# The first norm's weight as one row, spread over the partitions by TensorE, with the second half of x requested right behind it

## The chip, the cores and the metric

The kernel runs on one core of a Trainium2 chip. A core has TensorE (PE, matrix products), VectorE (DVE), ScalarE (ACT), GpSimd (POOL) and SyncE (SP), each with its own queue of instructions, taken in order. They meet through semaphores. SyncE writes the requests for all DMA transfers here. The metric is the time of one execution on the device, in microseconds, as the median of several runs.

## The reference

A decoder trunk of two layers over x with 256 tokens of width 1024, all in float32. The part that matters here is the first step of the first layer:

```python
def rms_norm(x, g):
    xf = x.astype(jnp.float32)
    y = xf * lax.rsqrt(jnp.mean(xf * xf, axis=-1, keepdims=True) + RMS_EPS)
    return (y * g.astype(jnp.float32)).astype(x.dtype)

for l in range(DEPTH):
    h = rms_norm(x, norm_mix[l])
    proj = h @ w_in[l]          # then three mixers (S5, NSA, stick-breaking), merge, output projection
    ...
    h = rms_norm(x, norm_ffn[l])
    x = x + conv_ffn(h, ...)
return rms_norm(x, norm_final)
```

`norm_mix[0]`, called the gain below, is a row of 1024 numbers by which every token's normed row is multiplied.

## The kernel before

Tokens lie on the 128 partitions, in two blocks t = 0 and 1 of 128 tokens; `xr[:, t, :]` holds a block's 1024 columns, in two halves h of 512. Each layer norms x into `xn`, transposes it on TensorE into `hh` and `hl` (each float32 value is split in a high part hh and a rest hl), and multiplies it by weight pieces that are split the same way into `wh` (ScalarE) and `wl` (VectorE). Weight chunks come through `ring`, three slots, each loaded again when VectorE has split what was in it. Every engine's order is written out by hand. `xn` and the gains are parts of one buffer, which the profile names `gate`.

At the start the order around the change is this.

SyncE requests the first half of x (block 0), the lambda rows (two requests) and step rows (two), the identity matrix (`kon`, 64 KB), the gain (`g_next`, read with a broadcast so that it lands on all 128 partitions, 512 KB), the second half of x (block 1), and then the chunks of the ring.

ScalarE squares a block as soon as it has landed and sums the squares (L1226), and takes the root (L1232). VectorE forms the bias of the root (`norm_bias`, L1562), waits for the lambda and step rows and spreads the latter (L1706), and norms the block (`norm_rows`: a reciprocal L1567, then for each half one scalar_tensor_tensor L1572, x times 1/root times gain). It does this for block 0, then block 1. Then it forms `hl` (L1578) and `wl` (L1556). The small computations for the S5 tables and the splits of further pieces come behind.

TensorE waits for the identity, runs ten products of the identity with itself into bank bY (`idle(10)`, L736, a warm-up whose results nobody reads), transposes block 0 when `xn_ready` says so (`turn_normed`, L795, banks bX0 and bX1), transposes the lambda rows (L820), runs four more such products, transposes block 1 (banks bA and bB), again four, and then starts the projection into the banks pj0 and pj1. A product of two plain float32 operands shows as two records in the profile, a transpose as one.

Of the kernel before, what the change touches and what calls it, by code (L numbers as in the profile page):

```python
# [20 lines left out]
ALU = mybir.AluOpType  # L21
# [3 lines left out]
P = 128  # L25
D = 1024
# [125 lines left out]
K_ID, K_ROT, K_TRI, K_NEG1 = 0, 128, 256, 384  # L152
# [72 lines left out]
def build(nc, x, norm_mix, w_in, ssm_lam_re, ssm_lam_im, ssm_log_step, ssm_b_re, ssm_b_im,  # L225
# [3 lines left out]
    with ExitStack() as ctx:  # L229
        def sb(name, shape, dtype=F32):  # L230
            return ctx.enter_context(nc.sbuf_tensor(name, shape, dtype))

        def bank(name):
            return ctx.enter_context(nc.psum_tensor(name, [P, 512], F32))
# [3 lines left out]
        def sem(name, per_round=0, start=0, rounds=DEPTH):  # L238
            t = Tally(ctx.enter_context(nc.semaphore(name)), name, per_round, start, rounds)
            tallies.append(t)  # L240
            return t
# [3 lines left out]
        kon = sb("kon", [P, K_ALL])  # L245
        xr = sb("xr", [P, NT, D])
# [7 lines left out]
        rstd = sb("rstd", [P, NT])  # L254
# [13 lines left out]
        kr = sb("kr", [P, 4, T])  # L268
# [42 lines left out]
                st[:, :, :].rearrange("p (c t) q -> p c (t q)", c=2)]  # L311
        s5xs = [s5x[:, :, :], bnat[:, :, :, :].rearrange("p c t i -> p c (t i)")]

        cv = work[:, 0]
        aT = work[:, 1]
        yt = work[:, 2]
# [23 lines left out]
        xn = gates[:, 2]  # L340
        g_next, g_ffn = gates[:, 1, 0], gates[:, 1, 1]
# [8 lines left out]
        pj = [bank(f"pj{i}") for i in range(2)]  # L350
# [3 lines left out]
        bB = bank("bB")  # L354
        bO = bank("bO")
        across_banks = [bX[0], bX[1], bA, bB]


        ident_in = sem("ident_in")
        consts_in = sem("consts_in")  # L360
        x_in = [sem(f"x_in{i}") for i in range(NT)]
        g_in = [sem(f"g_in{i}", 16, 16 if i else 0) for i in range(2)]
        setup = sem("setup")
        passed = sem("passed")
        out_sent = sem("out_sent")
# [153 lines left out]
        xd = x.rearrange("b (t p) d -> p (b t) d", p=P)  # L519
        od = out.rearrange("b (t p) d -> p (b t) d", p=P)  # L520

        def half(h):
            return slice(CH * h, CH * h + CH)
# [25 lines left out]
        @block.sync  # L549
        def _(sp):  # L550
            sp.dma_start(xr[:, 0, :], xd[:, 0, :]).then_inc(x_in[0].sem, 16)
            sp.wait_ge(setup.sem, 1)
            sp.sem_inc(passed.sem, 1)
            sp.dma_start(stP[L_RE:L_RE + DEPTH * ST, :], ssm_lam_re.rearrange("l (t w) p -> (l t) (w p)", w=2))\
# [3 lines left out]
            for l in range(DEPTH):  # L558
                sp.dma_start(lstep[L_ST + 32 * l:L_ST + 32 * l + ST, :],
                             ssm_log_step[l:l + 1].rearrange("l (t w) -> (l t) w", w=2)).then_inc(lam_in.sem, 16)  # L560
            sp.dma_start(kon[:, K_ID:K_ID + P], consts[:, K_ID:K_ID + P]).then_inc(ident_in.sem, 16)
            sp.dma_start(g_next, norm_mix[0:1, :].broadcast_to([P, D])).then_inc(g_in[1].sem, 16)
            sp.dma_start(xr[:, 1, :], xd[:, 1, :]).then_inc(x_in[1].sem, 16)

            def row(w, l):
                return w[bass.ds(l, 1)]
# [102 lines left out]
            for l in range(DEPTH):  # L669
# [34 lines left out]
                i = C_FFN  # L704
# [19 lines left out]
            n = 2 * DEPTH  # L724
# [9 lines left out]
        def _(pe):  # L734
            def mm(o, a, b, start, stop):
                return nc.tensor.matmul(o, a, b, start=start, stop=stop, skip_group_check=True)  # L736
# [62 lines left out]
            def turn_normed(n, t):  # L799
                for h in range(2):  # L800
                    pe.wait_ge(xn_ready.sem, xn_ready.at(n, 2 * t + h + 1))
                    turn(xn, t, h)
# [6 lines left out]
            def idle(n):  # L809

                for _ in range(n):
                    mm(bY[:, 0:P], ident, ident, True, True)

            pe.wait_ge(ident_in.sem, 16)
            idle(10)
            for l in range(DEPTH):
                turn_normed(2 * l, 0)
                if l == 0:
# [716 lines left out]
        def _(v):  # L1535
            TT, TS, STT = nc.vector.tensor_tensor, nc.vector.tensor_scalar, nc.vector.scalar_tensor_tensor

            for part in (stP, stA, stB, stC):
                nc.vector.memset(part, 0.0).then_inc(setup.sem, 1)
            nc.vector.memset(one[:, :], 1.0).then_inc(setup.sem, 1)  # L1540
# [24 lines left out]
            def norm_rows(n, t):  # L1565
                v.wait_ge(root_ready.sem, root_ready.at(n, t + 1))
                nc.vector.reciprocal(rstd[:, t:t + 1], rstd[:, t:t + 1]).then_inc(dve_step.sem, dve_step.up())  # L1567
                v.wait_ge(dve_step.sem, dve_step.last())
                g, gain = (g_in[0], g_ffn) if n % 2 else (g_in[1], g_next)
                v.wait_ge(g.sem, g.at(n // 2, 16) if n % 2 else g.at(n // 2, 0))  # L1570
                for h in range(2):
                    STT(xn[:, t, half(h)], xr[:, t, half(h)], rstd[:, t:t + 1], gain[:, half(h)], ALU.mult, ALU.mult)\  # L1572
                        .then_inc(xn_ready.sem, xn_ready.up())

            def turned_lo(l, n, t, h, k):
# [119 lines left out]
            for l in range(DEPTH):  # L1695
                n = 2 * l
# [5 lines left out]
                if l == 0:  # L1702
                    v.wait_ge(lam_in.sem, 64)
                    for w in range(DEPTH):
# [3 lines left out]
                            lstep[rows, :].rearrange("t (w o) -> t w o", o=1).broadcast_to([ST, 2, HD]))\  # L1708
                            .then_inc(step_row.sem, 1)
                norm_rows(n, 0)  # L1710
                if l:
                    x_down(l - 1, 1, 0)
# [4 lines left out]
                    split_lo(l, 2)  # L1717
                norm_bias(n, 1)
                norm_rows(n, 1)
                if l == 0:  # L1720
                    turned_lo(l, 1, 0, 0, 0)
# [182 lines left out]
                for q in range(SLOTS):  # L1904
                    f = q // 2
# [27 lines left out]
                    n = U_FILL + f  # L1933
# [15 lines left out]
                    if q in OS_SPLIT:  # L1949
                        n = OS_SPLIT[q]  # L1950
# [21 lines left out]
                n = 2 * l + 1  # L1972
# [6 lines left out]
                split_lo(l, S_FFN)  # L1979
                x_out(l, 0, 1)  # L1980
                norm_rows(n, 0)
                x_out(l, 1, 1)
                turned_lo(l, 9, 0, 0, 0)
# [60 lines left out]
            n = 2 * DEPTH  # L2044
# [184 lines left out]
```

## Time and profile before

| | us |
|---|---|
| median of 3 runs (993.08 to 993.66) | 993.47 |
| the profiled execution | 991.46 |
| its span, first to last instruction | 989.7 |
| TensorE busy | 953.2 |
| VectorE busy | 746.2 |
| ScalarE busy | 565.4 |
| GpSimd busy | 338.2 |

The page of the profile tells busy times and the chain that ended last. Its timeline gives, for each engine, the start and length of what it ran in microseconds from the span's start, and in brackets how long the engine sat idle before and what ended that. The windows tell busy times by stretch. Durations below are of the profiled execution.

### The profile page before, as it was taken

What the parts mean: (1) busy time and instruction counts of PE and PEld (TensorE: products, weight loads), DVE (VectorE), ACT (ScalarE), POOL (GpSimd) and SP (SyncE); (2) the same over time, 40 slices, a digit from 0 to 9 for tenths busy, and PEclk for the clock granted to TensorE, in tenths of its full rate; (3) what the DMA queues carried; (4) which work ended last, traced back from release to release, by engine and by line L of the source; (5) the groups of instructions that cost most, each with busy time, mean ns of one, the idle gap of its engine ahead of it and who ended that gap; (6) DMA issues with size and microseconds to landing.
All of it is one profiled execution on the core that took longest, in us unless ns stands there. A gap on an engine that the chain in (4) does not pass through costs nothing.

```text
span 989.7 us, 17232 instructions
## 1 busy us (share of the span) xinstructions
PE 953.2 (96%) x6447; PEld 819.5 (83%) x6447; DVE 746.2 (75%) x1240; ACT 565.4 (57%) x905; POOL 338.2 (34%) x267
## 2 busy tenths in 40 slices
PE   7899899999999999999999998999999999999997
PEld 6799666776878999999989986777777799999996
DVE  5989999995666776677865689999857676665666
ACT  6436665757454655555564466666664555555544
POOL 0111666671320563155401047568506001011010
PEclk9999999999999999999999999999999999999999
DMA  8963433344554765555468424233645345655551
GB/s 230 263 187 96 133 114 128 122 98 164 168 168 136 204 196 179 181 200 170 132 179 255 155 93 128 85 129 103 183 141 170 128 152 190 200 182 177 200 176 43
DMA packets 135864, 156.83 MB, mean 158 GB/s; under 512 B 16400, under 2 KB 103032, under 8 KB 135800
## 3 DMA queue, kind: packets, MB, share of 16 engines
q1 hardware_dynamic: 135800, 155.98, 50.7%
q8 instruction: 40, 0.66, 0.3%
q14 instruction: 24, 0.20, 0.1%
HBM read 154.92 MB, written 1.05 MB: 158 GB/s over the span
## 4 chain that ended last, share of the span: by engine, by line
PE 73%; DVE 16%; ACT 5%; issue 3%; POOL 2%; DMA 1%; SPq 0%; DVEq 0%; ACTq 0%; POOLq 0%; PEldq 0%
PE pj L736 52%; PE bX L736 6%; PE bA L736 5%; DVE wl L1556 5%; PE bB L736 4%; PE bY L1085 2%; DVE s5x L1885 1%; PE bY L736 1%; DVE work L1849 1%; DVE bnat L1885 1%; POOL s5h L2144 1%; PE bX L1074 1%; DVE gate L1572 1%; DVE hl L1578 1%; PE bO L736 1%
## 5 line engine op out<-in xcount | busy, mean ns | idle before, releaser
L1556 DVE TENSOR_TENSOR wl<-ring,wh 128x1024 fp32r<-128x1024 f32 (+1 forms) x276 | 365.0, 1326 | 136.4 <-ACT wh L1262 134.9
L1262 ACT ACTIVATE wh<-ring 128x1024 fp32r<-128x1024 f32 (+1 forms) x276 | 289.0, 1048 | 238.2 <-PE pj L736 201.4
L736 PE MATMUL pj<-hh,wh 128*128 128x256 f32 x1024 | 293.1, 286 | 6.7 <-DVE wl L1556 4.8
L736 PE MATMUL pj<-hl,wh 128*128 128x256 f32 x1024 | 289.7, 283 | 0.0
L736 PE MATMUL pj<-hh,wl 128*128 128x256 f32 x1024 | 289.7, 283 | 0.0
L736 PEld LDWEIGHTS pj<-hh,wh 128*128 128x128 f32 x1024 | 196.2, 192 | 11.3 <-issue 6.6
L736 PEld LDWEIGHTS pj<-hl,wh 128*128 128x128 f32 x1024 | 196.3, 192 | 1.2 <-issue 0.5
L736 PEld LDWEIGHTS pj<-hh,wl 128*128 128x128 f32 x1024 | 196.3, 192 | 0.0
L736 PE MATMUL pj<-wh,hl 128*128 128x512 f32 (+1 forms) x416 | 169.3, 407 | 10.3 <-ACT sbv L1249 4.9
L736 PE MATMUL pj<-wh,hh 128*128 128x512 f32 (+1 forms) x416 | 160.5, 386 | 0.0
L736 PE MATMUL pj<-wl,hh 128*128 128x512 f32 (+1 forms) x416 | 159.9, 384 | 0.0
L2182 POOL TENSOR_TENSOR work<-work 128x512 f32<-128x512 f32 x20 | 41.0, 2050 | 291.3 <-DVE work L1998 152.6
L736 PEld LDWEIGHTS pj<-wh,hl 128*128 128x128 f32 x416 | 78.5, 189 | 40.0 <-issue 11.3
L736 PEld LDWEIGHTS pj<-wh,hh 128*128 128x128 f32 x416 | 78.4, 188 | 16.4
L736 PEld LDWEIGHTS pj<-wl,hh 128*128 128x128 f32 x416 | 78.7, 189 | 12.8
L1998 DVE SCALAR_TENSOR_TENSOR work<-pj,par,work 128x254 f32<-128x254 f32 (+1 forms) x176 | 76.5, 475 | 13.4 <-ACT work L1480 8.3
L1480 ACT ACTIVATE work<-pj,par 128x256 f32<-128x256 f32 x88 | 44.2, 554 | 10.5 <-PE pj L736 10.5
L1351 ACT ACTIVATE work<-work,nm 128x128 f32<-128x128 f32 (+1 forms) x64 | 28.4, 444 | 31.4 <-DVE nm L1849 31.3
L2126 POOL TENSOR_TENSOR mr<-mr,work 128x512 f32<-128x512 f32 x16 | 31.9, 2008 | 32.7 <-DVE work L1614 32.7
L736 PE MATMUL bX<-wh,al 128*128 128x512 f32 x88 | 34.7, 395 | 0.3 <-DVE al L2033 0.3
L736 PE MATMUL bX<-wl,ah 128*128 128x512 f32 x88 | 34.5, 392 | 0.0
L736 PE MATMUL bX<-wh,ah 128*128 128x512 f32 x88 | 34.2, 389 | 0.0
(315 smaller groups left out, 1473.7 us busy)
## 6 DMA issues: line engine op xcount, KB each, us to landing
ring<-in_ffn_w_up SPq DMA_DIRECT2D x44, 1024.0 KB, 5.1
ring<-in_w_in SPq DMA_DIRECT2D x40, 1024.0 KB, 5.2
ring<-in_ffn_w_down SPq DMA_DIRECT2D x22, 1024.0 KB, 4.9
ring<-in_w_in SPq DMA_DIRECT2D x16, 512.0 KB, 5.3
ring<-in_w_branch SPq DMA_DIRECT2D x8, 1024.0 KB, 5.1
ring<-in_w_out SPq DMA_DIRECT2D x8, 1024.0 KB, 5.1
ring<-in_w_branch SPq DMA_DIRECT2D x8, 512.0 KB, 5.8
ring<-in_w_in SPq DMA_DIRECT2D x8, 256.0 KB, 5.1
```

The costliest lines, as they stand in the source:

```text
L736: return nc.tensor.matmul(o, a, b, start=start, stop=stop, skip_group_check=True)
L1074: ins = nc.tensor.matmul(bX[e][:, T * c:T * c + T], BL[r:r + 32, c, j, :], uT[r:r + 32, j, :], start=True, stop=True, skip_group_check=Tru ...
L1085: ins = nc.tensor.matmul(bY[r:r + 32, 0:T], w[:, j, r:r + 32], s5as[(4 * j + e) % 6][:, n, T * h:T * h + T], start=k == 0, stop=k == 3, sk ...
L1262: A(dst, src, ACT.Copy).then_inc(w_hi.sem, 1)
L1351: ins = A(p, p, ACT.Exp, bias=nm[:, m % 2, n:n + 1], scale=-1.0, accum_out=sm[:, m % 2, n:n + 1])
L1480: ins = A(cv[:, e, T * m:T * m + T], pj[n % 2][:, T * m:T * m + T], ACT.Identity, bias=par[:, 2, bass.ds(tile + (C_B + m), 1)], scale=par[ ...
L1556: TT(dst, src, hi.bitcast(F32), ALU.subtract).then_inc(w_lo.sem, 1)
L1572: STT(xn[:, t, half(h)], xr[:, t, half(h)], rstd[:, t:t + 1], gain[:, half(h)], ALU.mult, ALU.mult)\
L1885: ins = nc.vector.tensor_tensor_scan(g, decay, g, s5i[:, 2 + c:3 + c] if b else 0.0, ALU.mult, ALU.add)
L1998: ins = STT(dst, pj[n % 2][:, T * m:T * m + T - back], par[:, 1, bass.ds(tile + (col + m), 1)], dst, ALU.mult, ALU.add)
L2126: TT(m, m, yt[:, k % 2, :], ALU.add)\
L2182: TT(aT[:, cc % 2, :], cv[:, 0, :], cv[:, 1, :], ALU.mult).then_inc(a_ready.sem, 1)
```

## The change

The gain of the first norm is requested as one row onto partition 0 (4 KB). VectorE sets a row of 128 ones in `kr`, which is unused then, as its first instruction. TensorE, behind its ten warm-up products, multiplies the row of ones with the gain row, in two products of 512 columns, into pj0 and pj1; that puts the gain on all partitions. VectorE's first two normalisations read the gain from these banks, one half after the other. The later norms are as before. The identity, the gain row and the second half of x are requested directly behind the first half of x, ahead of the lambda and step rows.

```diff
+        ones_row = kr[0:1, 0, 0:P]
+        first_gain = [pj[0][:, :], pj[1][:, :]]
@@ sync
             sp.dma_start(xr[:, 0, :], xd[:, 0, :]).then_inc(x_in[0].sem, 16)
+            sp.dma_start(kon[:, K_ID:K_ID + P], consts[:, K_ID:K_ID + P]).then_inc(ident_in.sem, 16)
+            sp.dma_start(g_next[0:1, :], norm_mix[0:1, :]).then_inc(g_row.sem, 16)
+            sp.dma_start(xr[:, 1, :], xd[:, 1, :]).then_inc(x_in[1].sem, 16)
             sp.wait_ge(setup.sem, 1)
...
-            sp.dma_start(kon[:, K_ID:K_ID + P], consts[:, K_ID:K_ID + P]).then_inc(ident_in.sem, 16)
-            sp.dma_start(g_next, norm_mix[0:1, :].broadcast_to([P, D])).then_inc(g_in[1].sem, 16)
-            sp.dma_start(xr[:, 1, :], xd[:, 1, :]).then_inc(x_in[1].sem, 16)
@@ tensor
             pe.wait_ge(ident_in.sem, 16)
             idle(10)
+            pe.wait_ge(ones_set.sem, 1)
+            pe.wait_ge(g_row.sem, 16)
+            for h in range(2):
+                mm(first_gain[h], ones_row, g_next[0:1, half(h)], True, True).then_inc(g_spread.sem, 1)
@@ vector
+            nc.vector.memset(ones_row, 1.0).then_inc(ones_set.sem, 1)
@@ vector, norm_rows
-                v.wait_ge(g.sem, g.at(n // 2, 16) if n % 2 else g.at(n // 2, 0))
+                if n:
+                    v.wait_ge(g.sem, g.at(n // 2, 16 if n % 2 else 0))
                 for h in range(2):
-                    STT(xn[:, t, half(h)], xr[:, t, half(h)], rstd[:, t:t + 1], gain[:, half(h)], ALU.mult, ALU.mult)\
+                    if n == 0:
+                        v.wait_ge(g_spread.sem, h + 1)
+                    STT(xn[:, t, half(h)], xr[:, t, half(h)], rstd[:, t:t + 1], gain[:, half(h)] if n else first_gain[h],
+                        ALU.mult, ALU.mult)\
```

SyncE's requests at the start of the program, before the change. `st` and `lstep` take the lambda and step rows, `gate` the gain:

```order
L551 DMA xr<-in_x 128x1024
L554 DMA st<-in_ssm_lam_re 32x128 [waits setup]
L556 DMA st<-in_ssm_lam_im 32x128
L559 DMA lstep<-in_ssm_log_step 16x2 x2
L561 DMA kon<-in_consts 128x128
L562 DMA gate<-in_norm_mix 128x1024
L563 DMA xr<-in_x 128x1024
L593 DMA ring<-in_w_in 128x4x128 [waits w_lo]
```

And after it:

```order
L557 DMA xr<-in_x 128x1024
L558 DMA kon<-in_consts 128x128
L559 DMA gate<-in_norm_mix 1x1024
L560 DMA xr<-in_x 128x1024
L563 DMA st<-in_ssm_lam_re 32x128 [waits setup]
L565 DMA st<-in_ssm_lam_im 32x128
L568 DMA lstep<-in_ssm_log_step 16x2 x2
L599 DMA ring<-in_w_in 128x4x128 [waits w_lo]
```

Three requests have moved ahead of the four small ones, and the gain's is one row high.

TensorE's queue from its first instruction to the transposes of block 1, before:

```order
L736 MATMUL bY<-kon 128x128 [waits ident_in]
L736 MATMUL bY<-kon 128x128 x9
L795 MATMUL bX0<-kon,gate 128x128 [waits xn_ready]
L795 MATMUL bX0<-kon,gate 128x128 x3
L795 MATMUL bX1<-kon,gate 128x128 [waits xn_ready]
L795 MATMUL bX1<-kon,gate 128x128 x3
L820 MATMUL bO<-kon,st 128x128 [waits step_row]
L736 MATMUL bY<-kon 128x128 x4
L795 MATMUL bA<-kon,gate 128x128 [waits xn_ready]
```

And after:

```order
L742 MATMUL bY<-kon 128x128 [waits ident_in]
L742 MATMUL bY<-kon 128x128 x9
L742 MATMUL pj0<-gate,kr 128x512 [waits g_row,ones_set]
L742 MATMUL pj1<-gate,kr 128x512
L801 MATMUL bX0<-kon,gate 128x128 [waits xn_ready]
L801 MATMUL bX0<-kon,gate 128x128 x3
L801 MATMUL bX1<-kon,gate 128x128 [waits xn_ready]
L801 MATMUL bX1<-kon,gate 128x128 x3
L830 MATMUL bO<-kon,st 128x128 [waits step_row]
L742 MATMUL bY<-kon 128x128 x4
L801 MATMUL bA<-kon,gate 128x128 [waits xn_ready]
```

The two products that spread the gain stand between the ten warm-up products and the first transposes.

## Rows read from the trace of the kernel before

**Rows 1.** The page: busy time, share and instructions of each engine

```profile
PE 953.2 (96%) x6447; PEld 819.5 (83%) x6447; DVE 746.2 (75%) x1240; ACT 565.4 (57%) x905; POOL 338.2 (34%) x267
```

**Rows 2.** The chain of waits, first 13 us: start, length, what

```profile
4.05 5.49 DMA xr<-in_x
9.57 1.34 ACT gate L1226 x4
...
11.52 1.42 DVE gate L1572 x2
```

**Rows 3.** Timeline, SyncE: start us, length us, request [idle before]

```profile
0.81 0.39 SPq L551 DMA_DIRECT2D xr<-in_x  x1
...
3.12 0.42 SPq L561 DMA_DIRECT2D kon<-in_consts  x1
...
4.05 0.43 SPq L563 DMA_DIRECT2D xr<-in_x  x1
```

**Rows 4.** Timeline, VectorE, first 15 us

```profile
1.44 0.06 DVE L1540 MEMSET one<- 128x2 f32 x1
...
5.34 0.47 DVE L1706 COPY st<-lstep 16x128 f32<-16x128 f32 x2
...
8.34 1.42 DVE L1572 SCALAR_TENSOR_TENSOR gate<-xr,rstd,gate 128x512 f32<-128x512 f32 x2 [2.02 <-DMA gate<-in_norm_mix]
...
11.52 1.42 DVE L1572 SCALAR_TENSOR_TENSOR gate<-xr,rstd,gate 128x512 f32<-128x512 f32 x2
12.85 1.28 DVE L1578 TENSOR_TENSOR hl<-bX,hh 128x512 fp32r<-128x512 f32 x2
...
14.70 0.68 DVE L1578 TENSOR_TENSOR hl<-bA,hh 128x512 fp32r<-128x512 f32 x1
```

**Rows 5.** Timeline, TensorE's products; then its weight loads (min/median/max ns)

```profile
5.33 4.64 PE L736 MATMUL bY<-kon 128*128 128x128 f32 x20 [5.33 <-DMA kon<-in_consts]
9.76 1.56 PE L795 MATMUL bX<-kon,gate 128*128 128x128 f32 x8
...
L795 PEld LDWEIGHTS bX<-kon,gate x8: 140/230/230, 9.6 to 10.9; 128*128 128x128 f32 x8
```

**Rows 6.** Windows: stretch, length, busy time by engine, granted clock, DMA share, GB/s

```profile
8.00:10.00 2.00, 2.00 (x12) 2.00 (x11) 1.42 (x2) 0.43 (x1) 0.00 (x0) 1.00 1.11 340
...
20.00:30.00 10.00, 8.43 (x65) 7.76 (x64) 8.56 (x40) 7.85 (x14) 0.00 (x0) 1.00 0.82 190
30.00:40.00 10.00, 7.47 (x61) 7.12 (x60) 9.79 (x22) 4.26 (x5) 2.90 (x4) 1.00 0.97 228
```

**Rows 7.** Timeline, ScalarE

```profile
4.41 0.63 ACT L1226 ACTIVATE gate<-xr 128x512 f32<-128x512 f32 x1 [2.10 <-DMA xr<-in_x]
...
13.02 0.60 ACT L1238 ACTIVATE hh<-bA 128x512 fp32r<-128x512 f32 x1 [0.20 <-PE bA L795]
...
38.36 1.06 ACT L1262 ACTIVATE wh<-ring 128x1024 fp32r<-128x1024 f32 x1 [0.29 <-DMA ring<-in_w_in]
```

**Rows 8.** DMA requests of the start: count, KB each, median us to landing

```profile
lstep<-in_ssm_log_step SPq DMA_DIRECT2D x2, 0.1 KB, 2.5
```

**Rows 9.** Timeline around 53 us: float32 products and their reader

```profile
52.52 1.02 PE L736 MATMUL bO<-kr,kon 128*128 128x512 f32 x2
...
53.37 0.59 PE L736 MATMUL bX<-kr,kon 128*128 128x256 f32 x2
53.57 0.69 DVE L1765 TENSOR_TENSOR work<-bO,kon 128x512 f32<-128x512 f32 x1 [1.82 <-PE bO L736]
```

**Rows 10.** Two lines of VectorE: count, min/median/max ns, first and last start

```profile
L1572 DVE SCALAR_TENSOR_TENSOR gate<-xr,rstd,gate x4: 746/750/752, 8.3 to 12.2; 128x512 f32<-128x512 f32 x4
...
L1593 DVE SCALAR_TENSOR_TENSOR xr<-pj,xr x8: 682/687/691, 290.8 to 788.3; 128x512 f32<-128x512 f32 x8
```

**Rows 11.** Timeline, VectorE, the norm of the second layer

```profile
503.56 0.14 DVE L1562 TENSOR_SCALAR sbias<-ssum 128x1 f32<-128x1 f32 x1
...
504.27 1.41 DVE L1572 SCALAR_TENSOR_TENSOR gate<-xr,rstd,gate 128x512 f32<-128x512 f32 x2
```

More of the change, by code:

```diff
@@ L356, in build @@
         across_banks = [bX[0], bX[1], bA, bB]
+        first_gain = [pj[0][:, :], pj[1][:, :]]
         ident_in = sem("ident_in")
+        g_row = sem("g_row")
+        ones_set = sem("ones_set")
+        g_spread = sem("g_spread")
         consts_in = sem("consts_in")
         x_in = [sem(f"x_in{i}") for i in range(NT)]
-        g_in = [sem(f"g_in{i}", 16, 16 if i else 0) for i in range(2)]
+        g_in = [sem(f"g_in{i}", 16) for i in range(2)]
         setup = sem("setup")
```

## The prediction, made before the changed kernel was run

> **What bounds the kernel now.** The page comes first. TensorE is busy for 96% of the span [rows 1], but that average says little about an edit that touches only the first 13 us. So the second view is the chain of waits over that stretch. It runs back from the vector engine's second normalisation (11.52 us) to the second half of x, asked for at 4.05 us and landed 5.49 us later, and before that to SyncE, which spends its time writing DMA requests [rows 2]. The third view is the timeline of each queue. SyncE writes seven requests before that of x's second half [rows 3]; the gain row, copied to all partitions by its DMA (512 KB), is the seventh of them, and the identity the sixth. VectorE's first normalisation waits 2.02 us for that gain, and its second starts when the root of the second half is there [rows 4]. TensorE is not on this path, but it is not free either: it starts its ten warm-up products when the identity lands (5.33 us) and is through them at 9.76 us, when the first transposes start, although the first normed half had been there since about 9.1 us [rows 4, 5].
>
> From 13 to 49 us VectorE is the limit. Between 30 and 40 us it is busy for 9.79 of 10 us [rows 6], and everything it does there follows the second normalisation in its queue. After that TensorE carries the chain, each step waiting for its inputs. I find no fixed appointment behind 13 us. The ring's loads wait for VectorE's splits, so they move with it. A shift of the second normalisation should therefore reach the end whole.
>
> **The requests.** SyncE pays some 0.45 us for each [rows 3]. The identity moves from sixth to second (3.12 to about 1.26 us), the gain to third, x's second half to fourth: about 2.2 us in place of 4.05. The gain shrinks from 512 KB to 4 KB. The identity cannot be used before the first half of x has drained, since that is queued ahead of it: x was in at 4.38 us (ScalarE's start at 4.41 less a step) [rows 7], and 64 KB more at some 300 GB/s (the queues moved 340 GB/s between 8 and 10 us [rows 6]) is 0.2 us. I take TensorE's start as 4.6 us, 0.7 sooner than the 5.33 of before. The second half of x follows it, 512 KB at 300 GB/s or 1.7 us, at about 6.3 us in place of 9.54. The lambda and step rows are passed by all this. Their last request goes out at about 4.05 us, and with the 2.5 us that it took before [rows 8] they land by about 6.6 us, or 7 if they queue behind x. VectorE needs them before its first normalisation (two copies, 0.47 us), so without the gain it would be ready at about 7.6 us.
>
> **The gain's new way.** TensorE takes its instructions in order, and the two products that spread the row stand behind the ten warm-up products. That is the step that decides. The ten take 4.43 us (5.33 to 9.76) [rows 5], or 0.443 us for 128 columns. A product of two float32 operands with 512 columns takes 0.85 us in the trace (52.52 to 53.37, the start of the next product), which is 0.213 us for 128 columns [rows 9]. So the warm-up ran at half pace, 1.2 GHz against 2.4 GHz. The granted clock column reads 1.00 over the warm-up too [rows 6], so I read the level off the spacing. The transposes still load weights in 230 ns from 9.6 us on and reach 140 ns just before 11 us [rows 5], which puts the rise near 10.8 us, 5.5 us after TensorE's first product. The sum, with TensorE starting at 4.6 us:
> warm-up over at 4.6 + 4.43 = 9.05 us;
> the rise, 5.5 us after the start, at 10.1 us;
> first spreading product: 1.05 us at half pace does 0.52 us of its 0.85, the rest ends it at 10.43 us;
> second: 11.28 us. From the start of such a product to its reader is 1.05 us [rows 9], so 0.2 us more: the gain's halves are usable at 10.6 and 11.5 us, against 8.34 us for both before.
> The ends for this unknown: both products at half pace, 9.05 + 3.4 + 0.3 = 12.8 us; everything at full pace from TensorE's first product on, 4.6 + 2.2 + 1.7 + 0.2 = 8.7 us. The rows are nearer to the first, since half pace held in them for more than five microseconds.
>
> The Trainium skill ("TensorE: Matmul & The Clock Gate", section "What's actually happening") says that the moment of the rise is not tied to the kernel's start and moves by some ±500 ns between runs. By that, the second half of the gain would move by ±0.25 us. One execution cannot show it.
>
> **VectorE behind it.** The second half of the first block's normalisation starts at 11.5 us. A scalar_tensor_tensor that reads a bank takes 0.687 us where the present one from memory takes 0.750 us, and two vector reads of banks in a row take 1.28 us where two of the present ones take 1.42 us [rows 4, 10]. So each should be some 0.07 us shorter. The bias starts 0.6 us after it, at 12.1 us, and from bias to normalisation, with nothing else to wait for, is 0.71 us (503.56 to 504.27) [rows 11]: the second block's normalisation starts at 12.8 us. The pair takes 1.2 us in place of 1.33, and hl starts at 14.0 us, where it started at 12.85 us. That is **+1.15 us**.
>
> By the Trainium skill ("VectorE: DVE Perf Modes", section "The TRN2 errata") an operation whose source is PSUM has 120 fixed cycles of 0.96 GHz against 58 from SBUF, so the three on the path would be 0.2 us longer together instead of 0.2 us shorter. By that rule the shift would be +1.55 us. The durations in [rows 10] speak against it.
>
> **What is hidden.** TensorE transposes the first block later and then does its four warm-up products, until about 13.8 us, so the transposes of the second block start some 0.3 us after their input. ScalarE's copy of them ended at 13.6 us while VectorE took it up at 14.70 us [rows 4, 7]. The cover is over 1 us and holds. The added memset of one row is bounded by the 0.06 us of a tiny one [rows 4] in a stretch in which VectorE then waits for x; at worst 0.1 us. Its product waits for it, long done. The 508 KB less of DMA traffic frees about 1.7 us of the queues, but no weight chunk is waited for before 38.36 us, and there for 0.29 us [rows 7]. The bound of this is from 0 to -0.3 us, and I take 0.
>
> **The sum.** The profiled execution has 991.46 us with a span of 989.7 us; +1.15 makes 992.6 and 990.85 us. Its time stood 2.0 us under the median of the runs, 993.47 us. Carried over to that, the forecast is 993.47 + 1.15, or **994.6 us**.
>
> **The rivals.**
> *The rise comes late (slower).* Two things speak for it: before, the rise stood at 10.8 us on the span's own time, and no row shows products with a single row of weights, as the two new ones are, at the end of a warm-up. Should TensorE stay at half pace until both products are done, the gain's second half comes at 12.8 us, the second normalisation at 14.1 us and hl at 15.3 us: +2.4 us, 995.9 us. It decides from a rise at about 11.8 us on (+2.0 us: each microsecond of it costs half of one). For the forecast: before, the rise came 5.5 us after a start from which TensorE worked without a gap, and it will do so here too.
> *The gain is early enough (faster, though under the bound).* Should TensorE run at full pace from its first product, the gain's second half is there at 8.7 us, the bias at 9.3 us, the second normalisation at 10.0 us and hl at 11.2 us: -1.6 us, 991.9 us. The rows of the warm-up speak against it. If also the chunks of the ring came earlier by as much as their bound, it would be 991.5 us, at the bound of faster.
> *The shift is swallowed.* Between 20 and 30 us VectorE is busy for only 8.56 us [rows 6], since it waits for splits behind ScalarE and TensorE. If those gaps hung on something that does not move, part of the shift would vanish: 993.5 to 994.0 us. Against it: the waiting engines wait for VectorE's earlier output in their turn.
> *The late lambda rows.* They would have to land after 9.9 us, 5.8 us after their request where the 512 KB of x took 5.5, to matter. I count that with the first rival.
>
> **How the numbers follow.** A measurement of this kernel can tell 0.2% from no change, which is 2 us: below 991.5 us is faster, above 995.5 us slower. Forecast (993.9 to 995.4): 0.58. Late rise: 0.17, nearly all of it beyond the bound. Early gain: 0.10, of which a third beyond the bound. Swallowed: 0.10. Left over, for something that I don't see, 0.05, to both sides. That gives faster 0.05, same 0.77, slower 0.18. The range takes in the price of the late rise with 0.3 us above it, and stops short of half the early case: 992.4 to 996.2 us.
>
> **What would show it.** In the changed kernel's timeline: x's second half requested at about 2.2 us and squared from about 6.3 us; TensorE's first product at 4.6 us; the two products into pj from 9.05 us on; VectorE's first normalisation after a wait that ends with TensorE, at 10.6 us; the second at 12.8 us; hl at 14.0 us. In the chain of waits the DMA of x would be replaced by TensorE behind the identity's DMA. The prediction is wrong if the products into pj start before 8.5 us, if VectorE's second normalisation starts before 11.5 us, or if it starts late and the stretch from 49 us on doesn't show the same shift.

## The result, and the profile after

| | before | changed |
|---|---|---|
| median of 18 runs each, same chips, us | 992.98 (991.49 to 993.82) | 994.67 (993.34 to 997.33) |
| ratio, with its 95% interval | 1 | 1.0022 (1.0014 to 1.0030) |
| profiled execution, us | 991.46 | 996.85 |
| its span, us | 989.7 | 995.1 |

The change makes the kernel slower by 0.22%, some 2 us. The forecast was 994.6 us, and the median is 994.67 us. That the two agree so closely is partly luck: over all 18 runs the kernel before stood 0.5 us lower than in the three runs shown ahead of the prediction, so the shift was 1.7 us by the medians and 2.2 us by the ratio, where 1.15 us was forecast.

The profiled execution is 5.4 us behind that of before, more than twice the ratio, so it must not be read as the typical one. The times of the changed kernel fall into two groups, 13 of them from 993.3 to 995.1 us and 5 from 996.1 to 997.3 us. The profile is one of the five. Four of these, from 996.85 us up, have the profile's mean granted clock over the execution (0.996); the one at 996.08 us has 0.992, the lowest of all 18, so it probably went another way. The group matters for the ratio: the mean of all 18 runs is 2.2 us above that of the kernel before, the mean of the 13 alone 1.4 us. The changed kernel was profiled twice more for that reason (below).

The chain of waits of the changed kernel, from the start (start, length, what):

```profile
1.26 3.26 DMA kon<-in_consts
...
4.56 4.64 PE bY L742 x20
9.20 3.71 PE pj L742 x4
12.91 1.96 PE bX L801 x8
```

Where the chain of before consisted of the DMA of x's second half, ScalarE and VectorE [rows 2], it is now TensorE from the moment in which the identity lands: the ten warm-up products, the two spreading products (four records), the transposes. The timelines of SyncE, TensorE, ScalarE and VectorE tell the same, and answer to [rows 3, 4, 5, 7]:

```profile
2.10 0.35 SPq L560 DMA_DIRECT2D xr<-in_x  x1
7.06 0.63 ACT L1236 ACTIVATE gate<-xr 128x512 f32<-128x512 f32 x1 [0.97 <-DMA xr<-in_x]
...
7.82 0.47 DVE L1721 COPY st<-lstep 16x128 f32<-16x128 f32 x2 [2.56 <-DMA lstep<-in_ssm_log_step]
...
9.13 3.78 PE L742 MATMUL pj<-gate,kr 1*128 1x512 f32 x4
...
11.32 0.75 DVE L1586 SCALAR_TENSOR_TENSOR gate<-xr,rstd,pj 128x512 f32<-128x512 f32 x1 [2.83 <-PE pj L742]
...
12.94 0.75 DVE L1586 SCALAR_TENSOR_TENSOR gate<-xr,rstd,pj 128x512 f32<-128x512 f32 x1 [0.88 <-PE pj L742]
...
14.31 1.41 DVE L1586 SCALAR_TENSOR_TENSOR gate<-xr,rstd,pj 128x512 f32<-128x512 f32 x2
15.64 1.28 DVE L1593 TENSOR_TENSOR hl<-bX,hh 128x512 fp32r<-128x512 f32 x2
...
18.05 0.69 DVE L1593 TENSOR_TENSOR hl<-bA,hh 128x512 fp32r<-128x512 f32 x1 [0.48 <-ACT hh L1248]
```

x's second half is requested 2 us sooner and is in 2.5 us sooner, which is what the new order was to give. It buys nothing, since VectorE then waits 2.83 us for the first spreading product and 0.88 us for the second. These products run at half pace: 3.71 us for two in the chain, where 1.7 us is the price at full clock [rows 9]. The second normalisation starts at 14.31 us in place of 11.52. A second loss stands in the last row: VectorE waits 0.48 us for the copy of the second block's transposes, which had over 1 us in hand before.

A good mark for what the start costs is VectorE's first read of bank bO, behind the whole stretch up to 50 us in which VectorE had been the limit. In the kernel before and then in the changed one:

```profile
53.57 0.69 DVE L1765 TENSOR_TENSOR work<-bO,kon 128x512 f32<-128x512 f32 x1 [1.82 <-PE bO L736]
```

```profile
56.96 0.69 DVE L1780 TENSOR_TENSOR work<-bO,kon 128x512 f32<-128x512 f32 x1 [1.81 <-PE bO L742]
```

It is 3.4 us late in this execution. From there to the normalisation at about 300 us the delay grows to 5.1 us (302.73 to 307.83 us). The windows of the changed kernel show the cause, a stretch in which the granted clock fell (columns as in [rows 6]); in the profile of the kernel before, all windows between 100 and 140 us have 1.00:

```profile
122.00:126.00 4.00, 1.55 (x10) 1.21 (x9) 4.00 (x11) 3.19 (x11) 3.48 (x2) 1.00 0.17 25
126.00:130.00 4.00, 4.00 (x12) 2.59 (x12) 3.86 (x11) 2.46 (x7) 2.40 (x2) 0.57 0.69 253
```

TensorE was busy for only 1.55 of the 4 us ahead of the fall, waiting for VectorE. The same stretch of work exists in the kernel before, with TensorE as little busy, and there the clock stayed:

```profile
118.00:122.00 4.00, 1.57 (x13) 0.98 (x10) 4.00 (x12) 2.57 (x11) 3.35 (x2) 1.00 0.19 71
```

Whether the clock falls in it differs from execution to execution.

### The profile page after: what moved, and what is told of

Read it like the earlier page. It is cut to its first block, busy times and chain, and to the rows that moved or that the text cites. A ratio compares the mean times of both kernels' runs of the same rounds, so it can differ in the third digit from the quotient of the medians.

```text
span 995.1 us, 17242 instructions
## 1 busy us (share of the span) xinstructions
PE 959.7 (96%) x6451; PEld 822.5 (83%) x6451; DVE 746.6 (75%) x1241; ACT 565.8 (57%) x905; POOL 338.0 (34%) x267
## 4 chain that ended last, share of the span: by engine, by line
PE 74%; DVE 16%; ACT 5%; issue 3%; POOL 2%; DMA 0%; DVEq 0%; SPq 0%; ACTq 0%; POOLq 0%; PEldq 0%
PE pj L742 52%; PE bX L742 6%; PE bA L742 5%; DVE wl L1567 5%; PE bB L742 4%; PE bY L742 2%; PE bY L1095 1%; DVE s5x L1900 1%; DVE work L1864 1%; DVE bnat L1900 1%; POOL s5h L2159 1%; PE bX L1084 1%; PE bO L742 1%; DVE s5a L1804 1%; DVE mr L1889 1%
```

## The experiments

Every kernel ran beside the kernel before on one chip: 992.89 us median in the first group (e1 to e4), 992.68 in the second, 992.75 in the third. "Mark" is the start of the read of bO, 53.57 us in the first profile of the kernel before. Each kernel has one profile, unless said otherwise.

### The same kernels profiled again: e1, e2, e12

The kernels are unchanged.

> The changed kernel, unaltered, looked at once more. In its first profile the spreading products ran at half pace throughout, the second normalisation started at 14.3 us and VectorE's stretch up to 50 us was 3.4 us late; another 1.7 us were lost between 57 and 300 us, where the granted clock fell to 0.5 for 3.4 us at about 126 us of the span. Theory A (the early loss is the change's own; the dip at 126 us is chance of an execution): 3.4 us late at 50 us again give or take half a microsecond, dips elsewhere or fewer, and the end 1.7 us apart for each dip of 3.4 us. Rival B (the changed start brings the dip each time): a dip near 126 us again and the end 5 us behind.

> The kernel before, unaltered, looked at once more. Its first profile has one fall of the clock, at about 605 us. Theory A: the rise at the start and the number of falls differ from look to look, the rise within a microsecond or two of 10.8 us and the second normalisation at 11.5 us all the same, since it waits for x and not for TensorE. Rival B: the same rise, the same single fall.

> The changed kernel, looked at a third time, to see in which of its two ways it starts. Theory A (the clock is lost to the single-row products each time): either the rise comes only behind them, at 14 us or later, with the second normalisation at 14.3 us and the stretch at 50 us 3.2 to 3.4 us late, or it comes before and is lost again, with 12.3 us and 1.2 to 1.4 us late. Rival B (what the first two looks showed was chance): a rise before 11 us that stays.

| | before | e2 (before) | changed | e1 (changed) | e12 (changed) |
|---|---|---|---|---|---|
| time of the execution, us | 991.46 | 991.97 | 996.85 | 993.17 | 994.52 |
| second normalisation | 11.52 | 11.71 | 14.31 | 12.34 | 11.94 |
| hl of the first block | 12.85 | 13.04 | 15.64 | 13.66 | 13.26 |
| hl of the second block | 14.70 | 14.89 | 18.05 | 16.14 | 15.67 |
| mark | 53.57 | 53.76 | 56.96 | 55.00 | 54.68 |

The kernel before starts the same way twice. The changed one has at least two ways. In e1 and e12 the clock had risen when the spreading products ran, which therefore took 1.98 us in place of 3.78. But then it was taken back behind them. The products of e1, then its windows:

```profile
8.95 1.98 PE L742 MATMUL pj<-gate,kr 1*128 1x512 f32 x4
...
8.00:10.00 2.00, 2.00 (x10) 1.39 (x9) 0.49 (x3) 0.28 (x2) 0.00 (x0) 1.00 1.10 275
10.00:11.00 1.00, 0.93 (x4) 0.10 (x2) 0.78 (x2) 0.00 (x0) 0.00 (x0) 1.00 1.16 253
11.00:12.00 1.00, 0.89 (x6) 0.65 (x7) 0.78 (x2) 0.19 (x1) 0.00 (x0) 1.00 1.05 275
12.00:13.00 1.00, 1.00 (x7) 1.00 (x6) 0.83 (x2) 0.85 (x3) 0.00 (x0) 0.50 1.20 286
...
14.00:15.00 1.00, 1.00 (x6) 1.00 (x6) 1.00 (x3) 0.00 (x0) 0.00 (x0) 0.50 1.13 361
```

TensorE counts as busy for nearly all of the 8 to 12 us, with the spreading products in the middle, and still falls to 1.2 GHz at 12 us. So the transposes and the four warm-up products behind them run at half pace, ScalarE's copy of the second block comes late and VectorE waits 0.55 us for it. The mark moved by 3.3, 1.3 and 1.0 us in the three profiles, against the mean of the two of before. So theory A's "3.4 us late again" was wrong for e1, and so was B's end 5 us behind. The dip at 126 us was absent in e1 and there, a little sooner, in e12. In all three the clock was late or lost in the start, in one of the two ways that A named for e12, though e12 itself was a little earlier than A had it (11.94 us where 12.3 was expected, and 1.0 us late where 1.2 to 1.4 was).

### Taking the change apart: e3 and e4

e3 keeps the requests and leaves out the gain of the first norm (ones in its place):

```diff
-            sp.dma_start(g_next[0:1, :], norm_mix[0:1, :]).then_inc(g_row.sem, 16)
...
-            pe.wait_ge(ones_set.sem, 1)
-            pe.wait_ge(g_row.sem, 16)
-            for h in range(2):
-                mm(first_gain[h], ones_row, g_next[0:1, half(h)], True, True).then_inc(g_spread.sem, 1)
...
+            nc.vector.memset(g_next, 1.0).then_inc(g_spread.sem, 2)
```

> The changed kernel without the gain row's DMA and without the two spreading products: the gain of the first norm is left out, a memset of ones by VectorE stands in its place. It keeps the new order of requests. Theory A (the products behind the warm-up are the whole cost, the requests a gain): first normalisation 8.5 us, set by the step rows, the second 10.4 us, hl 11.7 us in place of 12.85; the end 1.1 us before that of the kernel before (992.0 where that has 993.1). Rival B (the requests cost something, as the step rows land at 7.8 us in place of 5.3 us): hl at 12.85 us or later, the end level or slower.

Measured: 992.19 us against 992.89, ratio 0.9995 (0.9986 to 1.0004); second normalisation at 9.65 us, hl at 10.98 us, mark at 51.72 us:

```profile
6.91 0.47 DVE L1716 COPY st<-lstep 16x128 f32<-16x128 f32 x2 [1.49 <-DMA lstep<-in_ssm_log_step]
...
9.65 1.41 DVE L1581 SCALAR_TENSOR_TENSOR gate<-xr,rstd,gate 128x512 f32<-128x512 f32 x2
```

The requests are a gain of 1.9 us at the mark, more than expected, since the step rows landed sooner than in the changed kernel. At the median only 0.5 to 0.7 us of it is left, and the interval touches no change. Of rival B (the requests cost), the late hl falls for this kernel; its level end is within the interval. From e3 to the changed kernel the ratio rises from 0.9995 to 1.0022, or 2.7 us, with some 1 us of uncertainty by the two intervals: the price of the spreading products at their place, and of the gain row's request, which e3 leaves out too.

e4 moves the three requests alone and keeps the gain at 512 KB:

```diff
             sp.dma_start(xr[:, 0, :], xd[:, 0, :]).then_inc(x_in[0].sem, 16)
+            sp.dma_start(kon[:, K_ID:K_ID + P], consts[:, K_ID:K_ID + P]).then_inc(ident_in.sem, 16)
+            sp.dma_start(g_next, norm_mix[0:1, :].broadcast_to([P, D])).then_inc(g_in[1].sem, 16)
+            sp.dma_start(xr[:, 1, :], xd[:, 1, :]).then_inc(x_in[1].sem, 16)
             sp.wait_ge(setup.sem, 1)
```

> The kernel before with the new order of requests alone: the gain still comes over all partitions by its 512 KB DMA, ahead of x's second half and of the lambda and step rows. Theory A: x's second half lands at about 8.5 us in place of 9.54, but the step rows queue behind it and land at 9 us; first normalisation 9.6 us, second 11.7 us: within 0.4 us of the kernel before. Rival B (the order of requests is what costs): more than 1 us slower.

Measured: 994.57 us against 992.89, ratio 1.0019 (1.0010 to 1.0028), a miss: it was expected within 0.4 us, and rival B's "more than 1 us slower" is what came. In this form, with the gain at 512 KB, the order of requests costs. The early part went as expected (second normalisation 11.43 us), but the mark is 54.27 us, 0.5 to 0.7 us late. The reason stands in two rows:

```profile
8.69 0.47 DVE L1706 COPY st<-lstep 16x128 f32<-16x128 f32 x2 [3.44 <-DMA lstep<-in_ssm_log_step]
...
10.20 1.77 PE L795 MATMUL bX<-kon,gate 128*128 128x128 f32 x8 [1.77 <-DVE gate L1572]
```

The step rows queue behind a megabyte and come at 8.69 in place of 5.34 us. TensorE, through its warm-up, stands idle for 1.77 us, and the clock, which had risen within the warm-up, falls at 10.9 us (granted 0.50 from 11 to 14 us). The transposes then run at half pace, and VectorE waits 0.57 us for ScalarE's copy of the second block, as in e1. So a start can lose the clock without any product over a single row, where TensorE stands idle. Where the rest of the 1.9 us goes I can't show; the profiled execution ended at 992.37 us, at the low end of e4's runs (992.27 to 995.48).

### The rows of the product: e5, e9, e10

e5 is the changed kernel with spreading products over all 128 rows:

```diff
-        ones_row = kr[0:1, 0, 0:P]
+        ones_row = kr[:, 0, 0:P]
...
-                mm(first_gain[h], ones_row, g_next[0:1, half(h)], True, True).then_inc(g_spread.sem, 1)
+                mm(first_gain[h], ones_row, g_next[:, half(h)], True, True).then_inc(g_spread.sem, 1)
...
-            nc.vector.memset(ones_row, 1.0).then_inc(ones_set.sem, 1)
+            nc.vector.memset(ones_row, 0.0).then_inc(ones_set.sem, 1)
+            v.wait_ge(ones_set.sem, 1)
+            nc.vector.memset(kr[0:1, 0, 0:P], 1.0).then_inc(ones_set.sem, 1)
...
+                    nc.gpsimd.memset(g_next, 0.0).then_inc(g_clear.sem, 1)
```

> The changed kernel with the two spreading products made over all 128 rows: the ones stand in row 0 of a 128x128 operand that is zero elsewhere, and the gain row above 127 rows of zeros; the products are as long as before, and the gain row is requested behind x's second half, when its place is cleared. Theory A (TensorE's clock isn't carried by products of a single row: in one look it rose only at 16.9 us, in the other it fell again behind them): the rise at 8.7 to 10.9 us and no fall before 50 us; second normalisation at 12.2 to 12.9 us, VectorE's stretch at 50 us 0.8 to 1.4 us late, the median 0.8 to 1.2 us over the kernel before, and no runs at 996 us or more. Rival B (only the length of the products and the phase of the rise matter): the same two levels as the changed kernel, median 1.7 to 2.2 us over the kernel before.

Measured: 993.70 us against 992.68, ratio 1.0007 (0.9999 to 1.0016), no run over 995.1 us. The weight loads show the rise between the second and the last of the spreading products, and it stays (start, length, x count):

```profile
9.94 0.34 PEld L745 LDWEIGHTS pj<-gate,kr 128*128 128x128 f32 x1 [0.52 <-issue]
10.79 0.19 PEld L745 LDWEIGHTS pj<-gate,kr 128*128 128x128 f32 x1 [0.52 <-issue]
...
13.14 0.97 PEld L745 LDWEIGHTS bY<-kon 128*128 128x128 f32 x8
```

Second normalisation 13.22 us (0.3 later than expected), mark 55.15 us, 1.5 us late and so just past the upper end of A's range. The group at 996 us is absent (0 of 12 runs, where the changed kernel has 5 of 18). And 4 of the 12 runs, at 991.9 to 992.4 us, have a mean granted clock of 0.997, which none of the changed kernel's 18 reaches. So theory A passes, though the row is requested later here too, and this execution had the fall of the clock near 125 us as well.

That other difference is absent in the pair e9 and e10: the kernel before with two products added that nobody reads, behind the ten warm-up products.

```diff
             idle(10)
+            pe.wait_ge(x_in[0].sem, 16)
+            for h in range(2):
+                mm(pj[h][:, :], kon[0:1, K_ID:K_ID + P], xr[0:1, 0, half(h)], True, True)
```

e10 has `ident` and `xr[:, 0, half(h)]` for the two operands.

> The kernel before with two more float32 products of 512 columns behind the ten warm-up products, over a single row (row 0 of the identity by row 0 of x), into pj0 and pj1, where nobody reads them; nothing waits for them but the transposes behind. Requests and gain as before. Theory A (single-row products don't bring TensorE's clock up): both at half pace, 9.7 to 13.2 us, the rise at 13.9 us or later, the first hl at 14.5 to 15 us, VectorE's stretch at 50 us (the read of bO) 2.5 to 3.4 us later than the 53.6 to 53.8 of before. Rival B (any product does): rise at 10.8 us, products through at 12.0 us, the stretch at 50 us within 0.6 us of before.

> The same with the same two products over all 128 rows (the identity by x). Theory A: rise at 8.7 to 10.9 us and no fall, products through at 11.3 to 12.0 us, first hl at 12.9 to 13.3 us, the stretch at 50 us 0 to 0.6 us later than before, and the median 1.5 to 2.5 us under that of the single-row sibling. Rival B: no difference between the two siblings beyond the interval.

In the profiles the pair differs as A said. TensorE in e9, then in e10:

```profile
9.74 3.78 PE L736 MATMUL pj<-xr,kon 1*128 1x512 f32 x4
...
15.42 1.91 PE L736 MATMUL bY<-kon 128*128 128x128 f32 x8
```

```profile
9.66 2.33 PE L736 MATMUL pj<-xr,kon 128*128 128x512 f32 x4
...
12.81 1.06 PE L736 MATMUL bY<-kon 128*128 128x128 f32 x8
```

With a single row the products and all behind them up to 17 us run at half pace, and the mark is 57.73 us (4.1 late, where A had 2.5 to 3.4). With 128 rows, of the same length in columns and starting 0.08 us apart, the clock rises within them and the mark is 53.78 us, as in the kernel before. The medians differ far less: 993.27 and 992.99 us against 992.75, ratios 1.0012 (1.0003 to 1.0021) and 1.0004 (0.9995 to 1.0013). There rival B was nearer, since I had expected 1.5 to 2.5 us between the siblings. The runs explain the gap: of the 11 of e9, three are at 995.6 us and eight at 992.6 to 993.4 us, of the 11 of e10 none is above 993.9. The profiled execution was among the three. So the single row costs some executions 2 to 3 us and the others little. But it costs those too: e10 has 3 runs at 991.8 us and the kernel before 12 of 27 at 992.0 us or less, each with a mean granted clock of 0.997, and e9 has none there. One profile of each could be an accident of when the clock rose; the missing low runs, 0 of 11 in e9 and 0 of 18 in the changed kernel, could hardly be.

### The place of the products: e6, e7, e8, e11

e6 has four warm-up products ahead of the spreading ones in place of ten; e7 has the spreading products ahead of the ten.

```diff
-            idle(10)
+            idle(4)
```

```diff
+            pe.wait_ge(ones_set.sem, 1)
+            pe.wait_ge(g_row.sem, 16)
+            for h in range(2):
+                mm(first_gain[h], ones_row, g_next[0:1, half(h)], True, True).then_inc(g_spread.sem, 1)
             pe.wait_ge(ident_in.sem, 16)
             idle(10)
```

> The changed kernel with four warm-up products ahead of the two spreading products in place of ten. Theory A (what the products wait for behind the warm-up is the cost): TensorE through the four at 6.3 us, the products at half pace until 9.8 us, first normalisation's second half 10.0 us, second normalisation 11.4 us, hl 12.6 us: 0.2 us before the kernel before; a late rise costs the transposes and products behind up to 0.5 us, so the end from -0.3 to +0.6 us. Rival B (the ten are needed for the clock): no gain against the changed kernel, +1.7 us or more.

> The changed kernel with the two spreading products ahead of the ten warm-up products. Theory A: the gain's halves usable at 6.0 and 7.8 us, first normalisation at 8.5 us (set by the step rows, landed at 7.8), second at 10.5 us; but the warm-up now ends at 11 to 12 us, and the first transposes behind it, hl at 13.1 us: +0.3 us. Rival B (the products' place doesn't matter, the requests cost): second normalisation no earlier than 11.5 us.

Measured: e6 994.22 us, ratio 1.0014 (1.0005 to 1.0023), second normalisation 11.77 us, mark 54.16 us. e7 992.73 us, ratio 1.0007 (0.9998 to 1.0017), second normalisation 10.18 us, hl 13.65 us behind the late transposes, mark 54.53 us. Against the first profile of the changed kernel, e6 has the products 2.5 us sooner and the normalisation too; e7 has the products 4.7 us sooner and the normalisation 4.1 us, since there the step rows and no longer the gain set it. So their place is the cost, as A said. For e6 the end is a miss (+1.5 us where -0.3 to +0.6 was expected) and near rival B's +1.7: the mark is 0.5 us late, and its profile shows a fall of the clock between 122 and 126 us (granted 0.62). Of the earlier start little was left at the end.

e8 puts all in the order of need: the gain row first, the small rows ahead of the identity and x's second half, the products ahead of four warm-up products.

```diff
+            sp.dma_start(g_next[0:1, :], norm_mix[0:1, :]).then_inc(g_row.sem, 16)
             sp.dma_start(xr[:, 0, :], xd[:, 0, :]).then_inc(x_in[0].sem, 16)
             sp.wait_ge(setup.sem, 1)
...
             for l in range(DEPTH):
                 sp.dma_start(lstep[L_ST + 32 * l:L_ST + 32 * l + ST, :],
...
+            sp.dma_start(kon[:, K_ID:K_ID + P], consts[:, K_ID:K_ID + P]).then_inc(ident_in.sem, 16)
+            sp.dma_start(xr[:, 1, :], xd[:, 1, :]).then_inc(x_in[1].sem, 16)
```

> All of it put in the order in which it is needed: the gain row is requested first of all, then x's first half, the lambda and step rows, the identity, x's second half; the spreading products stand ahead of the warm-up, and that is four products. Theory A: gain usable at 4.9 and 6.7 us, step rows in at 5.5 us, first normalisation at 6.8 us, second at 9.3 us (set by x's second half, landed at 7.5), hl at 10.6 us, 2.2 us before the kernel before; the clock rises late, which gives 0.5 us back: the end -1.7 us, 991.2 where the kernel before has 992.9. Rival B (at half pace everything behind is slower and eats the gain): level with the kernel before.

Measured: 991.54 us against 992.68, ratio 0.9986 (0.9977 to 0.9995). This one beats both kernels: 1.1 us under the kernel before by the medians and 1.4 us by the ratio, and by the two ratios 0.36% under the changed one. It had been expected 1.7 us under the kernel before, with the second normalisation 0.4 us sooner than it came. The chain is again the DMA of x's second half, 1.8 us sooner than in [rows 2]:

```profile
3.95 3.77 DMA xr<-in_x
...
7.74 1.34 ACT gate L1236 x4
...
9.69 1.41 DVE gate L1586 x2
11.10 1.20 DVE hl L1593 x2
```

TensorE does its spreading products from 2.35 to 6.0 us, at half pace, and it costs nothing there. The mark is 51.74 us. The transposes still run at half pace, 1.92 us for the eight from 7.90 us on. So 7 us after TensorE's first product the clock had not risen, where it had after 5.5 us in the kernel before, whose start has no product over a single row; e6, e7 and e11 are as late.

e11 asks for x first, the gain row second and the identity last of these, the rest as e8:

```diff
             sp.dma_start(xr[:, 0, :], xd[:, 0, :]).then_inc(x_in[0].sem, 16)
+            sp.dma_start(g_next[0:1, :], norm_mix[0:1, :]).then_inc(g_row.sem, 16)
             sp.wait_ge(setup.sem, 1)
...
+            sp.dma_start(xr[:, 1, :], xd[:, 1, :]).then_inc(x_in[1].sem, 16)
+            sp.dma_start(kon[:, K_ID:K_ID + P], consts[:, K_ID:K_ID + P]).then_inc(ident_in.sem, 16)
```

> The kernel that put all in the order of need, with the order mended once more: x's first half, the gain row, the lambda and step rows, x's second half, the identity. The spreading products stand ahead of four warm-up products. In its sibling the second normalisation started at 9.69 us, behind x's second half, in at 7.7 us. Theory A: x's second half in at 7.3 us, second normalisation at 9.3 us, hl at 10.6 us, 0.4 us before the sibling; the median 1.2 to 2.0 us under the kernel before. Rival B (behind the start something else is late already, such as the weight chunks or the clock): no better than the sibling's -1.1 to -1.4 us.

Measured: 992.64 us against 992.75, ratio 1.0006 (0.9997 to 1.0015). The expectation failed. The gain row now waits for x's 512 KB in the queues:

```profile
4.25 3.74 PE L742 MATMUL pj<-gate,kr 1*128 1x512 f32 x4 [4.25 <-DMA gate<-in_norm_mix]
7.92 2.07 PE L742 MATMUL bY<-kon 128*128 128x128 f32 x8
...
11.52 0.69 DVE L1593 TENSOR_TENSOR hl<-bX,hh 128x512 fp32r<-128x512 f32 x1 [0.71 <-ACT hh L1248]
```

The products start 1.9 us later than in e8. The second normalisation is at 9.40 us as hoped, but the transposes come behind TensorE's queue, so hl waits until 11.52 us and the mark is 52.72 us, 1.0 us behind e8. Asked for ahead of x, the row delayed x's first half by some 0.2 us (ScalarE takes it up at 4.63 us in e8 and 4.42 us in e11) and was itself usable 1.9 us sooner.

## Why the prediction was right, and where it was not

**The deciding step held.** That the spreading products stand behind the warm-up, that this runs at half pace, and that the gain therefore comes later than the DMA brought it, is what all three profiles show. TensorE started at 4.56 to 4.66 us (forecast 4.6), the products at 8.55 to 9.13 us (9.05). The request of x's second half went out at 2.10 us (2.2), and it was in at 6.7 to 7.1 us (6.3). The step rows were taken up at 7.5 to 7.9 us, where the forecast had them in by 7. Neither mattered, since the gain came later still, as the sum had it. e3, e7 and e8 take the products away or forward and the normalisation follows.

**The clock's rise.** The forecast put it at 10.1 us and the second normalisation at 12.8 us. The three profiles gave 14.31, 12.34 and 11.94 us: one beyond the end for "both at half pace" (14.1 us), two below the forecast. The rival "the rise comes late" was what the profiled execution did, and its price (+2.4 us at hl) was measured at +2.8 us. It was given 0.17; the upper group of the runs, to which that execution belongs, is 4 or 5 in 18. By the Trainium skill ("TensorE: Matmul & The Clock Gate", section "What's actually happening") the moment moves by ±500 ns. Here it lay between about 8 us (e12, within the warm-up, which took 3.99 us there in place of 4.64) and some 16.7 us (the first profile, within the transposes of the second block), so the measurement decides against so narrow a spread for this kernel.

**What the sum left out.** It assumed that a clock once risen stays. In e1 and e12 it fell at 12.0 and about 11.2 us, and this is the failed step, the paragraph on what is hidden: "the cover is over 1 us and holds". The four warm-up products took 1.9 us in place of 1.1 us, the copy of the second block came 0.5 us after VectorE was ready for it, and the shift against the two profiles of before grew from 0.7 and 0.3 us at hl of the first block to 1.3 and 0.9 us at that of the second. So the mark at +1.0 to +1.3 us in the common case agrees with the forecast of 1.15, out of a smaller first term and a term that was put at zero. That agreement is luck too. The prediction had named as a sign of being wrong a late normalisation whose shift the stretch from 49 us on doesn't repeat; in all three profiles the mark is later than the normalisation by another 0.6 to 0.7 us, so this sign did show.

**VectorE's reads of a bank.** I had taken 0.07 us off for each, and by an estimate from the fixed cycles that the Trainium skill gives ("VectorE: DVE Perf Modes", section "The TRN2 errata") each would have cost 0.065 us more. Neither came:

```profile
L1586 DVE SCALAR_TENSOR_TENSOR gate<-xr,rstd,gate x16: 744/750/755, 307.8 to 991.9; 128x512 f32<-128x512 f32 x16
L1586 DVE SCALAR_TENSOR_TENSOR gate<-xr,rstd,pj x4: 740/746/748, 11.3 to 15.0; 128x512 f32<-128x512 f32 x4
```

The 0.687 us of [rows 10] belongs to an instruction whose scalar is a constant, while this one reads rstd from memory. That this is the difference is my reading; no run separates it. The other row used for the term, two reads of banks in 1.28 us, is of tensor_tensor, which has no scalar from memory either. The term was worth 0.2 us.

**Carrying the shift to the end.** Nothing swallowed it: from the mark to the end e1 keeps 1.2 us of its 1.2 against e2, span against span. In between, the shift is 1.0 us at one normalisation (304.20 against 303.17 us) and 1.3 us at the next (307.89 against 306.62 us), which waits 0.27 us behind its reciprocal in all three profiles of the changed kernel and in neither of before; why, no run shows. But there are falls of the clock at about 125 us in some executions and not in others (the second layer has the same stretch at about 605 us; both profiles of before, e1 and e3 have a fall only there, e4, e9 and e10 only at the first), and such a fall is worth 1.7 us: from the mark to about 305 us, e5, which had the first of them, lost 1.7 us against e1, which hadn't. The kernel before has two levels as well, about such a fall apart: the 35 runs beside e5 to e8 lie at 991.3 to 991.9 us and at 992.5 to 993.9 us, with none between. The mean granted clock agrees in every one of them: 0.997 in the 13 lower runs, as in the profiles with one such fall, and 0.995 or 0.996 in the 22 upper ones.

This adds to the spread of both kernels. It is not what lifts the shift by the ratio, 2.2 us, above the early shift of the common profiles: among the 13 lower runs of the changed kernel 8 have the lower clocks (0.993 or 0.994, at 994.2 us and more, as e12 with its fall in the start and two later ones) and 5 have 0.995 (as e1 with one later fall), while beside them the kernel before has 13 of 18 in its upper level, so the later falls seem no more frequent. The late rise does most of it: without the five upper runs the means are 1.4 us apart, near the +1.0 to +1.3 us of the mark. To settle whether the changed start has a small effect on the falls would take many profiles of each kernel.

**The chances.** The range held the median. "Within 0.2%" had 0.77, and the ratio of 1.0022 lies just on the other side of that bound, with an interval over both. Had the late rise been given 4 or 5 in 18 and the lost clock behind the products a price, more of the chance would have stood on slower.

## What to carry to other kernels

An engine that looks free for a small helper is free only where nothing stands ahead of it in its queue: put such work ahead of the warm-up, with a request for its input that goes out before the large ones, and then take away as much warm-up as the work itself lasts. Each small request that is moved behind a large one arrives with the large one, so order requests by when they are needed and by size. And where a profile stands far from the median ratio, profile twice more before explaining its difference.

## What the runs showed of the hardware

TensorE's clock was not brought up, and not kept up, by float32 products over a single row. In the first profile of the changed kernel, e6 and e9 it was at 1.2 GHz all through them and the first block's transposes behind; in e1 and e12 it was at 2.4 GHz in them and fell behind them, with TensorE busy for 3.8 of the 4 us from 8 to 12 us in e1. The same products over 128 rows (e5, e10) had the rise within them, and the runs of e9 and e10 agree with the profiles. What is open is whether a start that has its rise early would have kept the clock behind products over 128 rows: neither e5 nor e10 was profiled with so early a rise. Two such products over a single row took 3.8 us at the one level and 2.0 us at the other.

TensorE's clock also fell where TensorE was little busy: at 10.9 us in e4 after 1.77 us without work, and at about 125 us in some executions after 1.55 of 4 us of work, though not in the kernel before after 1.57 of 4.

Requests of 0.1 KB that landed after 2.5 us [rows 8] took 4.5 us with a megabyte requested ahead of them (e4):

```profile
lstep<-in_ssm_log_step SPq DMA_DIRECT2D x2, 0.1 KB, 4.5
```
